# Reworked RMS norms, constants on another queue, and earlier page reads in a two-layer trunk kernel

## What is computed

```
def _rms(x, g):
    y = xf * rsqrt(mean(xf * xf, axis=-1) + EPS)
    return y * g

for layer in range(2):
    hp, hs = _rms(xp, norm_mix_g[layer]), _rms(xs, norm_mix_g[layer])
    op, os_ = gmlp_mix(...) if layer == 0 else sparse_attention(...)
    xp, xs = xp + op, xs + os_
    xp = xp + peer(_rms(xp, norm_ffn_g[layer]), ...)
    xs = xs + peer(_rms(xs, norm_ffn_g[layer]), ...)

# sample attention: scores of each of 8 samples against 2048 cached keys and one new one
ki_past = cik[page_table]            # 16 pages of 128 keys a sample
score = sum_h(relu(qi . ki) * wi);   keep the best 256;   softmax(q . k) v over those
```

## Time and profile before

| what | value |
|---|---|
| median of 3 runs | 3812.09 us |
| lowest, highest | 3808.44, 3823.56 us |
| the profiled execution's own time | 3846.35 us |
| its span | 3844.5 us |
| busy: TensorE, VectorE, ScalarE, GpSimd | 93%, 64%, 35%, 49% |
| DMA | 812.70 MB, 211 GB/s over the span |

### The profile page before, as it was taken

The page is one execution under the profiler, slowest core; times in us unless marked ns, Lnnn a source line. Parts: engine busy times, 40 slices in busy tenths (PEclk is TensorE's granted clock), DMA queues, the critical chain, the costliest instruction groups (busy, mean ns, idle before and its releaser), DMA issues.

```text
span 3844.5 us, 61950 instructions
## 1 busy us (share of the span) xinstructions
PE 3594.2 (93%) x21581; PEld 3414.4 (89%) x21581; DVE 2455.4 (64%) x5409; ACT 1358.1 (35%) x1905; POOL 1873.4 (49%) x1186
## 2 busy tenths in 40 slices
PE   7999999999999999999889488999999999999998
PEld 7998998999999999998853257999999999999998
DVE  2332297778775777775556642297877775777774
ACT  3322243535343333333221243244444443333332
POOL 3433366565655555553530132366565655555551
PEclk9999999999999999999999589999999999999999
DMA  3222267777778999983146131267777878989992
GB/s 120 83 68 76 92 186 253 261 247 278 265 274 278 300 319 313 325 284 97 66 124 183 52 100 45 87 197 232 275 245 265 268 274 269 306 298 327 313 309 99
DMA packets 373934, 812.70 MB, mean 211 GB/s; under 512 B 33592, under 2 KB 231160, under 8 KB 366472
## 3 DMA queue, kind: packets, MB, share of 16 engines
q1 hardware_dynamic: 157808, 455.78, 35.2%
q0 software_dynamic: 64208, 229.53, 17.6%
q10 hardware_dynamic: 151696, 124.51, 10.9%
HBM read 696.97 MB, written 112.74 MB: 211 GB/s over the span
## 4 chain that ended last, share of the span: by engine, by line
PE 69%; DVE 16%; DMA 5%; issue 4%; ACT 2%; POOL 2%; ACTq 0%; SPq 0%; another core or an unknown queue 0%; DVEq 0%; POOLq 0%
PE acc L587 42%; PE acc L574 15%; PE misc L718 3%; DMA rows<-u_in,expertP 3%; DVE rows L1678 2%; DMA raw<-slabs_in 2%; DVE hot_gate L1716 1%; POOL w_lo L2092 1%; PE misc L979 1%; DVE route L1617 1%; DVE misc L1613 1%; ACT w_hi L1041 1%; PE misc L758 1%; PE misc L597 1%; PE acc L968 1%
## 5 line engine op out<-in xcount | busy, mean ns | idle before, releaser
L2092 POOL TENSOR_TENSOR w_lo<-raw,w_hi 128x1024 fp32r<-128x1024 f32 x368 | 898.5, 2443 | 993.0 <-ACT w_hi L1041 992.2
L587 PE MATMUL acc<-h_hi,w_hi 128*128 128x416 f32 x3072 | 1095.8, 357 | 2.3 <-POOL h_lo L2143 1.3
L587 PE MATMUL acc<-h_lo,w_hi 128*128 128x416 f32 x3072 | 1083.8, 353 | 0.0
L587 PE MATMUL acc<-h_hi,w_lo 128*128 128x416 f32 x3072 | 1078.7, 351 | 0.0
L1041 ACT ACTIVATE w_hi<-raw 128x1024 fp32r<-128x1024 f32 x620 | 656.5, 1060 | 1182.7 <-DMA raw<-slabs_in 1136.5
L587 PEld LDWEIGHTS acc<-h_hi,w_hi 128*128 128x128 f32 x3072 | 579.4, 189 | 11.4 <-POOL h_lo L2143 1.6
L587 PEld LDWEIGHTS acc<-h_hi,w_lo 128*128 128x128 f32 x3072 | 580.4, 189 | 7.2
L587 PEld LDWEIGHTS acc<-h_lo,w_hi 128*128 128x128 f32 x3072 | 579.8, 189 | 3.9
L1795 DVE TENSOR_TENSOR w_lo<-raw,w_hi 128x1024 fp32r<-128x1024 f32 x252 | 329.4, 1307 | 203.8 <-ACT w_hi L1041 202.8
L1678 DVE CUSTOM_DVE_ANT_0 rows<-acc,rows 128x1024 f32<-128x1024 f32 (+1 forms) x224 | 273.6, 1223 | 205.5 <-DMA rows<-u_in,expertP 184.7
L587 PE MATMUL acc<-y_hi,w_hi 128*128 128x416 f32 x1024 | 361.4, 353 | 9.6 <-DVE y_lo L1787 4.3
(11 more groups left out here) (338 smaller groups left out, 5379.6 us busy)
## 6 DMA issues: line engine op xcount, KB each, us to landing
raw<-slabs_in SPq DMA_DIRECT2D x620, 512.0 KB
act_d<-gelu SPq DMA_DIRECT2D x256, 208.0 KB
gate_d<-gout SPq DMA_DIRECT2D x52, 1024.0 KB
abuf<-act_d ACTq DMA_DIRECT2D x32, 1664.0 KB, 14.9
gbuf<-gate_d ACTq DMA_DIRECT2D x30, 1664.0 KB
unit<-ck_in SPq DMA_DIRECT2D x64, 160.0 KB, 3.0
unit<-ck_in ACTq DMA_DIRECT2D x64, 160.0 KB, 3.1
vquad<-cv_in SPq DMA_DIRECT2D x64, 128.0 KB
```

The costliest lines, as they stand in the source:

```text
L587: last = pe.matmul(acc[:, 0, par, 0:ND], w[:, c, :], m(c), start=c == 0 and w is w_hi[r] and m is m_hi, stop=c == KC - 1 and w is w_lo[r])
L2092: pool.tensor_tensor(w_lo[r][:], raw[r][:], w_hi[r][:].bitcast(F32), ALU.subtract).then_inc(lo_done, 1)
```

## The change

Five edits:

- **Sum of squares.** VectorE adds the eight squared chunks into one tensor `ssum` (the buffer `ms`), seven adds, each after the square of its chunk (`add_square`). Those of `norm(0)` stand ahead of it, those of `norm(1)` after x6 and x7, those of `norm(2)` and `norm(3)` after x5, x6 and x7. TensorE does one product of `ones` with `ssum` (two matmuls).
- **Root from PSUM.** ScalarE takes the root from `misc[:, 0:2]` with scale 1/1024 and a bias tensor that holds eps. `ms_done` and the VectorE step are gone. The reciprocal is written to PSUM `misc[:, 2:4]` (`rstdB`), and the products read it there.
- **Start.** x comes in two DMAs of four chunks. ScalarE issues only `ones` and `gains`, does the squares (chunks 0 to 3 after `x_first`), then the two splits, then the root. The 12 other DMAs are issued by SyncE behind the first four slabs.
- **Page numbers.** In `load_unit`, on SyncE and on ScalarE, the four page numbers are read into registers ahead of the wait on `unit_used`.
- **Index matmuls.** Two go to a step over the first 12 steps, where three went to a step over the first 8.

```diff
-            sp.dma_start(x[:], a["xT"]).then_inc(x_loaded, 16)
+            sp.dma_start(x[:, 0:4], a["xT"][:, 0:4]).then_inc(x_first, 16)
+            sp.dma_start(x[:, 4:8], a["xT"][:, 4:8]).then_inc(x_loaded, 16)
             for r in range(4):
                 load(r, r)
+            sp.dma_start(ident[:], a["ident"]).then_inc(loaded, 16)
...
+            sp.dma_start(sel_p[:], a["sel_p"]).then_inc(loaded, 16)
             def load_unit(u, b):
+                pages = [page(b, u, j) for j in range(UNIT)]
                 sp.wait_ge(unit_used, u * TS + (b + 1))
                 for j in range(UNIT):
-                    sp.dma_start(unit[b % 4][:, j, :], a["ck"][bass.ds(page(b, u, j), 1)].squeeze(0)).then_inc(
+                    sp.dma_start(unit[b % 4][:, j, :], a["ck"][bass.ds(pages[j], 1)].squeeze(0)).then_inc(
                         unit_loaded[b % 4], 16)
@@ tensor
             def norm(k):
-                for c in range(KC):
-                    pe.wait_ge(sq_done, k * KC + c + 1)
-                    for half in range(2):
-                        last = pe.matmul(misc[:, half, 0:HT], ones[:], sq[:, c, half * HT:(half + 1) * HT],
-                                         start=c == 0, stop=c == KC - 1)
+                pe.wait_ge(ssum_done, (k + 1) * (KC - 1))
+                for half in range(2):
+                    last = pe.matmul(misc[:, half, 0:HT], ones[:], ssum[:, half * HT:(half + 1) * HT],
+                                     start=True, stop=True)
                 last.then_inc(sumsq_done, 1)
...
-                    if k < IH:
-                        for i in range(3):
-                            index_of(3 * k + i)
+                    for i in range(2 * k, 2 * k + 2):
+                        if i < 3 * IH:
+                            index_of(i)
@@ scalar
                     if x_ready is not None:
                         act.wait_ge(*x_ready(c))
+                    elif c == 0:
+                        act.wait_ge(x_first, 16)
+                    elif c == 4:
+                        act.wait_ge(x_loaded, 48)
                     act.activation(sq[:, c, :], x[:, c, :], ACT.Square).then_inc(sq_done, 1)
-                act.wait_ge(ms_done, k + 1)
-                act.activation(rms[:], ms[:], ACT.Sqrt).then_inc(rms_done, 1)
+                if x_ready is None:
+                    split(0, 0, first=True)
+                    split(0, 1, first=True)
+                    act.wait_ge(eps_ready, 1)
+                act.wait_ge(sumsq_done, k + 1)
+                act.activation(rms[:].rearrange("p (h t) -> p h t", h=2), misc[:, 0:2, 0:HT], ACT.Sqrt, bias=eps,
+                               scale=1.0 / D).then_inc(rms_done, 1)
...
-            act.dma_start(ident[:], a["ident"]).then_inc(loaded, 16)
...
-            split(0, 0, first=True)
-            split(0, 1, first=True)
-            act.wait_ge(x_loaded, 48)
             norm(0, None)
@@ vector
             def norm(k):
-                dve.wait_ge(sumsq_done, k + 1)
-                dve.tensor_scalar(ms[:].rearrange("p (h t) -> p h t", h=2), misc[:, 0:2, 0:HT], 1.0 / D, EPS,
-                                  ALU.mult, ALU.add).then_inc(ms_done, 1)
                 dve.wait_ge(rms_done, k + 1)
-                dve.reciprocal(rstd[:], rms[:]).then_inc(rstd_done, 1)
+                dve.reciprocal(rstdB, halves(rms[:])).then_inc(rstd_done, 1)
                 dve.wait_ge(rstd_done, k + 1)
                 for c in range(0, KC, 2):
                     for d in range(2):
-                        dve.scalar_tensor_tensor(sq[:, c + d, :], x[:, c + d, :], gains[:, k, c + d:c + d + 1], rstd[:],
-                                                 ALU.mult, ALU.mult).then_inc(hf_done, 1)
+                        dve.scalar_tensor_tensor(halves(sq[:, c + d, :]), halves(x[:, c + d, :]),
+                                                 gains[:, k, c + d:c + d + 1], rstdB, ALU.mult,
+                                                 ALU.mult).then_inc(hf_done, 1)
...
+            rstdB = misc[:, 2:4, 0:HT]
...
+            def add_square(k, c):
+                dve.wait_ge(sq_done, k * KC + c + 1)
+                if c > 1:
+                    dve.wait_ge(ssum_done, k * (KC - 1) + c - 1)
+                dve.tensor_tensor(ssum[:], sq[:, 0, :] if c == 1 else ssum[:], sq[:, c, :], ALU.add).then_inc(ssum_done, 1)
...
+                for c in range(1, 7) if m == 6 else (range(7, 8) if m == 7 else ()):
+                    add_square(1, c)
...
+                    if l < LAST_L and n >= NK - 3:
+                        for c in range(1, 6) if n == NK - 3 else range(c, c + 1):
+                            add_square(2, c)
...
+                    for c in range(1, 6) if m == 5 else (range(m, m + 1) if m > 5 else ()):
+                        add_square(3, c)
```

37 lines of the change are left out of this document (22 added, 15 removed).

## The result

The changed kernel takes 3772.31 us (median of 4 runs, 3770.58 to 3782.33), the one before, run beside it, 3815.64 us (3808.44 to 3823.56, 4 runs). The ratio is 0.9886, 95% interval 0.9873 to 0.9898: 43.3 us faster, 39 to 48 by the interval. The forecast was 3770.4. The profiled execution took 3770.58 us, span 3768.8.

A forecast was written before the change was run, and what follows sets the result against it. TensorE's long row of slab matmuls, 69% of the span, bounds the kernel. Terms 13.5 + 7.5 + 1.5 + 6.2 + 13 = 41.7 us, off the median 3812.09, gave 3770.4; spread 3760 to 3782, with A and B 3756 to 3792.

The forecast's parts named there:

- Ladder: In each norm, products reading the reciprocal from PSUM are no longer held up by GpSimd's h_lo: 3.0 us per norm.
- The sum, norm 1: Norm after w_out: VectorE adds, four matmul records and root from PSUM end the reciprocal 4.45 us earlier.
- Norms 2 and 3: Norms after y0 and ao: adds held by w_lo delay x7, leaving gains of 1.5 and 6.2 us.
- Start: First norm: split x, constants issued by SyncE and squares first save 13.5 us, range 9 to 15.5.
- two splits and the table load end at 14.7, beneath it: First norm: ScalarE's splits and table load finish while the sum is still being formed, so they add no time.
- term of 1.7 for a second slow stretch of TensorE: First slab at the start: denser operands avoid a second slow stretch of TensorE, saving 1.7 us.
- Index matmuls: Cache steps: two index matmuls a step instead of three avoid TensorE's waits on ScalarE's relus, saving 11 us.
- Page numbers: Cache steps: page reads ahead of the wait save 2.0 of the 3.45 us spent waiting for pages.
- A: Cache steps: ScalarE sets the pace, so the index work gains little; that part 2, time 3781; chance 0.14.
- B: Norms: PSUM does not cure the VectorE and GpSimd hold-up; 14.2 us less gain, time 3785; chance 0.14.
- C: Slabs after norms: fewer matmuls before the stall keep TensorE's clock low, 4.6 us a slab; time 3825; chance 0.04.
- D: Later phases: slab loads or gathers set their time and absorb the gains; time 3805; chance 0.06.

The follow-up runs named there:

- e1: Changed kernel with the reciprocal written to SBUF again and the VectorE products reading it there; ratio to the kernel before 0.9928.
- e2: Changed kernel with the index matmuls three to a step over 8 steps again, page reads still ahead of the wait; ratio to the kernel before 0.9929.
- e3: Changed kernel with the page reads behind the wait on unit_used again on both queues; ratio to the kernel before 0.9910.
- e8: Changed kernel with the root's table load ahead of the first norm's wait and ScalarE's next page reads ahead of taking the products; ratio to the kernel before 0.9909.
- r2: Changed kernel with the two later norms' adds placed later in VectorE's order, plus the two moves of e8; ratio to the kernel before 0.9880.
- r3: r2 with 8 extra matmuls of ones with ones ahead of each norm's wait on the sum; ratio to the kernel before 0.9876.
- e6: Changed kernel with extra TensorE matmuls in the norms, 16 ahead of the sum's wait and 40 behind (24 in the first); ratio to the kernel before 0.9900.
- r1: Changed kernel itself, unaltered, measured again on the chip of r2 and r3; ratio to the kernel before 0.9893.
- r4: The kernel before, unaltered, profiled once more in one run; its attention loop took 138.0 us from first to last start.
- e4: Changed kernel with the sum of squares on TensorE again, 16 matmuls and no VectorE adds; ratio to the kernel before 0.9894.
- e5: Changed kernel with the old start: x in one piece, 12 constants issued by ScalarE, splits ahead of the squares; ratio to the kernel before 0.9945.

## Why the prediction was right, and where it was not

- **Ladder.** Forecast 3.0 us a norm from products that GpSimd no longer holds up. Measured from the reciprocal's end to the slab's end: 13.7 before and 10.8 after in norms 1 and 3, 2.9 us, and 3.2 at the start (14.9 and 11.7); e1 shows the cause.
- **The sum, norm 1.** Forecast 4.45. From the start of x7 to the reciprocal's end it went from 11.8 to 8.4 us, 3.4. The mis-sized term is "four records at 0.22 each and a tail": 1.05 forecast, 2.10 measured, because I took the pace of 32 records at full clock for four that come after a stand. Where they took 1.14 us (e2, e3) the whole term is 4.35. Norm 1 in all: 7.5 forecast, 6.3 measured.
- **Norms 2 and 3.** The hold-up of the adds by `w_lo` was forecast from the earlier trace rows and came: x7 late by 3.5 us (4.1 forecast) and 1.1 (1.25), TensorE held by the tables to 1792.5, 15.3 us after the slab's end (15.7 forecast). The gains are 1.8 against 1.5, and 5.2 against 6.2; the missing 1.0 is again the sum, 2.10 us for 1.05.
- **Start.** Forecast 13.5, measured 10.7 at the first slab's end (11.9 at the last copy of that phase: 125.8 against 137.7). The failed step is "two splits and the table load end at 14.7, beneath it": the load for the root waits for the sum like the root, 1.3 us, of which e8 gives back 1.2. The other 1.5 us are the term of 1.7 for a second slow stretch of TensorE: from the reciprocal's end to the slab's end the start gained 3.2 us, the ladder's 3.0 and 0.2 more. The last `h_lo` takes 2.26 us there beside VectorE's mask product and 2.16 in the kernel before, so nothing was gained at it. The constants did not hold TensorE, as forecast.
- **Index matmuls.** Forecast 11, measured 12.2 by e2. The waits were all at the third matmul, as I argued.
- **Page numbers.** Forecast 2.0, measured 0 to 1.2. The step that failed is that earlier reads take 2.0 of the 3.45 us away: they took the small waits, and larger ones came in their place, 3.0 us in the changed kernel against 3.4 in e3. The bracket "after taking products ScalarE comes late to its reads" was the cause of those: with it mended 0 to 0.5 us are left of 1.5 to 3.9 (e8, r2, r3), and the change doesn't touch it. No run has e8's reads without the ones ahead of the wait.
- **Rivals.** A falls by e2, B by e1. C: the low clock costs 1.0 us at a sum and nothing behind it (e6), where C needed 4.6 a slab. D: nothing of size was given back behind the places; the gain stands in the total.
- **The total.** 43.3 us against 41.7 looks better than the terms were, and that nearness is luck: the five lengths sum to 36.6. The other 6.7 us lie in the long phases: behind norm 3 the span has 1434.7 us in the changed kernel and 1443.2 before, but 1444.9 in r1 and 1434.1 to 1450.5 over all traces. I don't count them as the change's. On the other chip the medians differ by 37.5 us (the ratio gives 41), and the lengths of r1 and r4 by 38.2. The prediction's own spread of 3760 to 3782 was also too narrow for its terms: its lowest sum, 21.6, gives 3790.

## What to carry to other kernels

When an engine runs its instructions in order, ask for each moved or added one what stands behind it: here five adds delayed the residual sum that released 15 DMAs, and moving them by one step gave 3.7 us, 0.7 of them from a shorter sum. Where VectorE works beside GpSimd, putting one of two operands into PSUM was worth 10 us over four norms (e1), more than a sum of 4 records in place of 32 (5.3, e4). A table load that could stand before a wait cost its 1.3 us behind it; a page read moved ahead of a wait brought 1.2 us at most, and moved further, ahead of the work that delayed it, it left 0 to 0.5 us of waits where there had been 1.5 to 3.9.

## What was not expected of the hardware

- In the changed kernel's norm 1 the granted clock fell in the sum, in e2's it did not: the same four records took 2.10 us (granted clock 0.50 over them) and 1.14 us (1.00), behind the same slabs and after stands of 2.20 and 2.23 us. In norm 3 they took 1.14 us after a stand of 3.34 in e2 and 2.10 after 3.25 in the changed kernel. The stand alone does not say which of the two comes, and what does stays open.

```profile
340.89 1.14 PE L614 MATMUL misc<-ms,ones 128*128 128x260 f32 x4 [2.23 <-DVE ms L1486]
2328.50 1.14 PE L614 MATMUL misc<-ms,ones 128*128 128x260 f32 x4 [3.34 <-DVE ms L1486]
```

- VectorE operations with two SBUF operands grow beside a GpSimd operation: a pair of products went from 1.43 to 2.47 us, an add from 0.70 to 2.02, and one in e5 to 2.65.
- The attention loop takes either about 109 or about 140 us in the same code, and with it the whole kernel is some 30 us longer.
